# A hybrid decoder layer on one core: gate pieces moved between the recurrence levels, squares summed on TensorE, and a turned tile copied ahead of its unit

## The reference, cut to what matters

```python
x = x + 0.5 * swiglu(rms_norm(x, ffn1[0]), ...)        # d_ff = 2816
y = mixer_block(rms_norm(x, mix[0]), ...)
x = x + y
x = x + 0.5 * swiglu(rms_norm(x, ffn2[0]), ...)

# mixer_block
q, k, v, iq, ik, iw, hq, hf, hi, hg, ga, gb = split(h @ w_in)
attn = attend(q, k, v, iq, ik, iw)        # indexer picks 128 or 256 keys, softmax over these
o = hgrn2(silu(hq), sigmoid(-hf), log f, hi, s0)       # gated linear recurrence, 4 heads of 128 x 128
o = rms_norm(o) * silu(hg)
merged = sigmoid(ga) * (attn @ w_proj_attn) + sigmoid(gb) * (o @ w_proj_hgrn)
y = merged @ w_out
```

## Time and profile before

| | |
|---|---|
| three timed runs | 1734.11, 1739.26, 1740.22 us; median 1739.26 |
| the profiled execution, its own time | 1732.57 us |
| its span | 1730.5 us |
| mean granted clock of TensorE | 0.982 of full speed |
| busy: PE, PEld, DVE, ACT, POOL | 95%, 87%, 42%, 26%, 40% |
| chain that ended last | PE 89%, DVE 4%, ACT 2%, DMA 2% |
| HBM over the span | 116 GB/s |

### The profile page before, as it was taken

The page is one execution under the profiler, slowest core; times in us unless marked ns, Lnnn a source line. Parts: engine busy times, 40 slices in busy tenths (PEclk is TensorE's granted clock), DMA queues, the critical chain, the costliest instruction groups (busy, mean ns, idle before and its releaser), DMA issues.

```text
span 1730.5 us, 29178 instructions
## 1 busy us (share of the span) xinstructions
PE 1646.1 (95%) x12749; PEld 1512.9 (87%) x12753; DVE 732.0 (42%) x1190; ACT 445.7 (26%) x629; POOL 697.0 (40%) x584
## 2 busy tenths in 40 slices
PE   7999999999998899967999999998999999999998
PEld 6999999999957899956888765657999999999998
DVE  6323012334316589478574644435643222022311
ACT  4112111212452224300233333332233111111211
POOL 4333444446321245655144342341443434443432
PEclk9999999999999999988899999999999999999999
DMA  6222233423411223201522277998223222322222
GB/s 180 74 73 76 84 104 98 116 76 108 159 30 40 66 98 90 81 27 51 174 77 80 77 268 274 422 411 331 74 74 91 80 66 84 103 78 74 83 68 89
DMA packets 193502, 203.59 MB, mean 118 GB/s; under 512 B 6224, under 2 KB 179344, under 8 KB 184928
## 3 DMA queue, kind: packets, MB, share of 16 engines
q1 hardware_dynamic: 173040, 105.56, 21.3%
q0 software_dynamic: 12832, 80.29, 12.3%
q10 hardware_dynamic: 7504, 15.88, 2.4%
HBM read 187.21 MB, written 14.30 MB: 116 GB/s over the span
## 4 chain that ended last, share of the span: by engine, by line
PE 89%; DVE 4%; ACT 2%; DMA 2%; issue 1%; POOL 1%; ACTq 0%; SPq 0%; DVEq 0%; POOLq 0%
PE ps L1596 25%; PE ps L1597 24%; PE ps L1598 24%; PE ps L2048 3%; PE ps L2065 1%; PE ps L2123 1%; PE ps L1994 1%; DMA k_page<-in_cache_k,kv_row 1%; PE ps L2012 1%; PE ps L2003 1%; PE ps L1926 1%; DVE k_lev L1302 1%; DVE n_lo L1024 1%; PE ps L1609 1%; DVE att L1282 1%
## 5 line engine op out<-in xcount | busy, mean ns | idle before, releaser
L489 POOL TENSOR_TENSOR w_lo<-raw,w_hi 128x512 fp32r<-128x512 f32 (+1 forms) x398 | 525.9, 1351 | 784.1 <-ACT w_hi L642 784.1
L1596 PE MATMUL ps<-n_lo,w_hi 128*128 128x288 f32 x1824 | 544.0, 298 | 1.0 <-ACT qT L748 1.0
L1597 PE MATMUL ps<-n_hi,w_lo 128*128 128x288 f32 x1824 | 538.6, 295 | 0.0
L1598 PE MATMUL ps<-n_hi,w_hi 128*128 128x288 f32 x1824 | 536.8, 294 | 0.0
L1596 PEld LDWEIGHTS ps<-n_lo,w_hi 128*128 128x128 f32 x1824 | 342.4, 188 | 15.5 <-issue 14.4
L1598 PEld LDWEIGHTS ps<-n_hi,w_hi 128*128 128x128 f32 x1824 | 344.0, 189 | 0.0
L1597 PEld LDWEIGHTS ps<-n_hi,w_lo 128*128 128x128 f32 x1824 | 343.0, 188 | 0.1
L642 ACT ACTIVATE w_hi<-raw 128x2048 fp32r<-128x2048 f32 (+2 forms) x108 | 188.0, 1740 | 268.5 <-PE ps L1598 268.4
L1597 PE MATMUL ps<-hid_hi,w_lo 128*128 128x288 f32 x704 | 208.4, 296 | 0.0
L1596 PE MATMUL ps<-hid_lo,w_hi 128*128 128x288 f32 x704 | 208.4, 296 | 0.0
L1598 PE MATMUL ps<-hid_hi,w_hi 128*128 128x288 f32 x704 | 208.1, 296 | 0.0
(11 more groups left out here) (302 smaller groups left out, 2278.2 us busy)
## 6 DMA issues: line engine op xcount, KB each, us to landing
raw<-in_ffn_w_gate SPq DMA_DIRECT2D x44, 512.0 KB, 3.9
raw<-in_ffn_w_up SPq DMA_DIRECT2D x44, 512.0 KB, 5.2
raw<-in_ffn_w_down SPq DMA_DIRECT2D x32, 704.0 KB, 4.7
raw<-in_w_in SPq DMA_DIRECT2D x22, 1024.0 KB, 5.3
gates<-scratch_g ACTq DMA_DIRECT2D x4, 1152.0 KB, 9.8
raw<-in_w_out SPq DMA_DIRECT2D x4, 1024.0 KB, 5.1
scratch_g<-g_ring POOLq DMA_DIRECT2D x7, 576.0 KB, 3.1
scratch_x<-xT ACTq DMA_DIRECT2D x1, 2304.0 KB, 11.9
```

The source lines that it names most:

```text
L489: ins = pool.tensor_tensor(w_lo[:, u % NRAW, part], raw[:, u % NRAW, part], w_hi[:, u % NW, part].bitcast(F32), ALU.subtract)
L1596: pe.matmul(dst, hi, x_lo, start=first, stop=False)
L1597: pe.matmul(dst, lo, x_hi, start=False, stop=False)
L1598: return pe.matmul(dst, hi, x_hi, start=False, stop=last)
```

## The change

Five things are done, all in the order of instructions.

1. **Pieces between levels.** The 8 pieces of gate units 0 and 1 move from `prompt_attention` into the levels of `heads`: after each level of both heads PE makes half a piece (12 matmuls) in PSUM banks 0 to 3. ACT copies them out at the head of its `heads(g)`, SP stores them unscaled, and POOL scales that quarter (the last of the four, by `gate_quarter`) at the end, after it was loaded back. What stays in `prompt_attention` is two pieces ahead, a whole one in each of steps 0 to 13, and half a piece in each of steps 14 to 29.
2. **POOL's order.** `w_lo` of gate unit 1 is made after `decays(0)`, that of unit 2 after `decays(1)`, that of unit 3 after the last state store.
3. **The search.** Five of its rounds move from steps 11 to 15 to DVE's `heads(0)`, behind the first `level_in`.
4. **Squares.** PE adds up the squares of x itself: for every chunk two products with a matrix of ones, between the matmuls of `first_unit`. DVE's eight instructions on `sqsum` go, and PE's `norm(0)` too.
5. **Turned tile first.** In ACT's `token_major` the first turned tile of unit i-1 is copied before ACT waits for unit i, the second right after the stage copies and before `split`.

The diff, cut to its core:

```diff
+def gate_quarter(n):
+    return (n // 2 + 3) % 4
...
+        PRE, FULL = 2, 14
+        def piece_of_step(n):
+            return (2 * HB + PRE + n, (0, 1)) if n < FULL else (2 * HB + PRE + FULL + (n - FULL) // 2, ((n - FULL) % 2,))
         @block.sync
+            def store_piece(i):
+                sp.wait_ge(S("gate_out"), i + 1)
+                at = i % 4 * HT
+                sp.dma_start(g_home(i // 4)[:, at:at + HT], g_piece(i)).then_inc(S(f"head_stored{i % 3}"), 16)
             for u in range(NRAW, U):
+                n = u - NRAW - at_unit["gate", 0]
+                if n in (0, 1):
+                    for i in range(4 * n, 4 * n + 3):
+                        store_piece(i)
                 load_unit(u)
+                if n in (0, 1):
+                    store_piece(4 * n + 3)
         @block.gpsimd
-            lows(at_unit["feat", 5] + 2)
+            lows(at_unit["gate", 0])
...
             for g in range(2):
                 decays(g)
+                lows(at_unit["gate", g + 1])
                 state_store(2 * g)
                 state_store(2 * g + 1)
+            lows(at_unit["gate", 3])
             attention_pages()
...
+                pool.wait_ge(S("quarter_in3"), X_IN[3] + 16)
+                at = GATES_AT[3]
+                for n in range(2):
+                    for a in range(2):
+                        part = gates[:, at + n, a, :]
+                        ins = pool.tensor_tensor(part, part, rms[:, :], ALU.mult)
+                ins.then_inc(S("gate_scaled"), 1)
         @block.scalar
             def token_major():
                 for i in range(2, NTOK):
+                    if i > 2:
+                        turn_copies(TURNS_OF[i - 1][0:1])
                     act.wait_ge(S("unit_done"), u + 1)
...
                     ins.then_inc(S("stage_done"), 1)
+                    if i > 2:
+                        turn_copies(TURNS_OF[i - 1][1:])
                     split(u + 2)
                     if i == 2:
                         index()
-                    if i != 2:
-                        turn_out(i - 1)
+                    if i > 2:
+                        stored_out(i - 1)
             def heads(g):
+                for i in range(4 * g, 4 * g + 4):
+                    gate_out(i)
+            def stored_out(i):
+                act.wait_ge(S("tok_done"), i + 1)
+                for dst, src in stores(i):
+                    act.dma_start(dst, src).then_inc(S(f"stored{i % 2}"), 16)
             def gate_out(i):
...
+                if i % 4 == 3:
+                    split(at_unit["gate", n] + 2)
         @block.vector
-                for c in range(DC):
-                    sq_add(0, c)
...
+                        if h == 0 and L == 1:
+                            take(EARLY)
                         level_out(a, L - 1)
...
-                    if n < 16:
+                    if n < 16 - EARLY:
                         take(1)
         @block.tensor
             def first_unit(u):
+                def square(c):
+                    pe.wait_ge(S("sq_done"), c + 1)
+                    for h in range(2):
+                        ins = pe.matmul(ps[:, SS_BANK[0] + h, 0:HT], ones, sq[:, c % 2, h * HT:(h + 1) * HT],
+                                        start=c == 0, stop=c == DC - 1)
+                    ins.then_inc(S("sq_summed" if c < DC - 1 else "ss_done"), 1)
...
+                        if turn == 1 and k >= 2:
+                            square(k - 2)
+                        if turn == 2 and k < 2:
+                            square(DC - 2 + k)
             def second_unit(hi, lo):
-                norm(0)
-            def gate_half(i):
+            def gate_piece(i, part):
...
-                for k in range(DC):
+                for k in range(DC // 2 * part[0], DC // 2 * part[-1] + DC // 2):
             def heads(g):
                 for L in range(len(LEVELS)):
...
                         ins.then_inc(S(f"level_done{a}"), 1)
+                    gate_piece(4 * g + L // 2, (L % 2,))
             def prompt_attention():
-                    if n + 2 < 4 * HA:
-                        gate_half(n + 2)
+                    if piece_of_step(n)[0] < PIECES:
+                        gate_piece(*piece_of_step(n))
```

More of the change, by code:

```diff
@@ L82, in weight_units @@
         w_in("feat", 3 * g + 2, OHG + 256 * g, 256)
-    for g in range(DC // 2):
-        w_in("gate", 2 * g, OGA + 256 * g, 256)
-        w_in("gate", 2 * g + 1, OGB + 256 * g, 256)
+    for n in range(DC):
+        q = gate_quarter(n)
+        w_in("gate", n, (OGB if n % 2 else OGA) + 256 * q, 256)
     for g in range(DC // 2):
@@ L437, in build @@
         SMALL_IN = 16 * 8
+        X_IN = (32, 16, 16, 16)
         SCORE_AT = {2: 0, 3: 256, 4: 640}
@@ L525, in attention_pages @@
                 value_group(6)
-                for n in range(8):
+                for n in range(2, 8):
                     lows(min(at_unit["gate", n] + 2, at_unit["proj", 0]))
                     if n == 6:
-                        pool.wait_ge(S("gate_stored1"), 48)
+                        pool.wait_ge(S("gate_stored1"), 32)
                         value_group(5)
                     if n == 7:
-                        pool.wait_ge(S("gate_stored0"), 64)
+                        pool.wait_ge(S("gate_stored0"), 48)
                         value_group(4)
@@ L650, in squared @@
             def squared(k, c):
-                if DC * k + c >= 2:
-                    act.wait_ge(S("sq_added"), DC * k + c - 1)
+                n = DC * (k - 1) + c
+                if k == 0 and c >= 2:
+                    act.wait_ge(S("sq_summed"), c - 1)
+                if n >= 2:
+                    act.wait_ge(S("sq_added"), n - 1)
                 act.activation(sq[:, c % 2, :], xT[:, c, :], ACT.Square).then_inc(S("sq_done"), 1)
@@ L830, in gate_out @@
             def gate_out(i):
-                n, at = i // 4, i % 4 * HT
-                if i % 4 == 0:
-                    split(at_unit["gate", n] + 1)
+                n = i // 4
                 if i % 4 == 3:
@@ L885, in prompt_attention @@
                         turned(n - 1)
-                    if n + 1 < 4 * HA:
-                        gate_out(n + 1)
+                    if n == 0:
+                        gate_out(2 * HB + 1)
+                    elif piece_of_step(n - 1)[1][-1] == 1 and piece_of_step(n - 1)[0] < PIECES:
+                        gate_out(piece_of_step(n - 1)[0])
                     if n == 4 * HA - 1:
@@ L898, in prompt_attention @@
                 turned(4 * HA - 1)
-                split(at_unit["gate", 7] + 2)
             def sample_attention():
@@ L991, in _ @@
                     act.wait_ge(S("v_used"), 4 * (25 + g))
+                if g == 3:
+                    for m in range(3):
+                        act.wait_ge(S(f"head_stored{m}"), 16 * len(range(m, 2 * HB, 3)))
                 at = GATES_AT[g]
                 act.dma_start(gates[:, at:at + 2, :, :].rearrange("p n a t -> p n (a t)"),
-                              scratch_g[2 * g:2 * g + 2].rearrange("n p t -> p n t")).then_inc(S(f"gates_back{g}"), 16)
+                              scratch_g[2 * g:2 * g + 2].rearrange("n p t -> p n t")).then_inc(S(f"quarter_in{g}"), 16)
             act.dma_start(xT[:, :, :].rearrange("p c t -> p (c t)"), scratch_x).then_inc(S("x_back"), 16)
@@ L1181, in _ @@
             taken = [0]
+            EARLY = 5
             def take_half():
@@ L1573, in _ @@
             features(0)
-            while taken[0] < 2 * ROUNDS - 4 * HA:
+            while taken[0] < 2 * (ROUNDS - 16):
                 take_half()
@@ L1890, in features @@
                     ins.then_inc(S("unit_done"), 1)
-            def gate_half(i):
+            def gate_piece(i, part):
                 n, a, t = i // 4, i // 2 % 2, i % 2
                 hi, lo = unit(at_unit["gate", n])
-                if i >= 2:
-                    pe.wait_ge(S("gate_out"), i - 1)
-                for k in range(DC):
+                head = i < 2 * HB
+                if part[0] == 0 and i >= 4:
+                    pe.wait_ge(S("gate_out"), i - 3 if head else i - 1)
+                bank = i % 4 if head else 6 + t
+                for k in range(DC // 2 * part[0], DC // 2 * part[-1] + DC // 2):
                     at = k * 256 + a * P
-                    ins = product(ps[:, 6 + t, 0:HT], hi[:, at:at + P], lo[:, at:at + P],
+                    ins = product(ps[:, bank, 0:HT], hi[:, at:at + P], lo[:, at:at + P],
                                   n_hi[:, k, t * HT:(t + 1) * HT], n_lo[:, k, t * HT:(t + 1) * HT],
                                   k == 0, k == DC - 1)
-                ins.then_inc(S("unit_done" if i % 4 == 3 else "gate_half"), 1)
+                if part[-1] == 1:
+                    ins.then_inc(S("unit_done" if i % 4 == 3 else "gate_half"), 1)
             def heads(g):
```

61 lines of the change are left out of this document (37 added, 24 removed).

## The result

The changed kernel takes 1729.36 us in the median of four runs (1728.46 to 1729.93). The kernel before, timed beside it, takes 1739.74 (1734.11 to 1741.01). The ratio is 0.994, with a 95% interval of 0.9914 to 0.9967: 10.4 us faster, where 22.7 were forecast, and outside the forecast range of 1705 to 1728.

What follows compares the result with a forecast made beforehand. The prediction took TensorE (PE), 89% of the chain, as the bound. Terms 2.0 - 14.3 + 9.6 + 2.0 - 22.0 gave -22.7 us, taking the median 1739.26 to 1716.5 us, range 1705 to 1728.

Steps and rivals of the forecast that it cites:

- squares, up to the first token turn: First unit: PE's products with ones replace the 3.44 us wait but delay the second unit, +2.0 us (+1.0 to +4.1).
- turned tiles, units 3 to 5: Token units: three PE waits shrink from 3.72 to 0.95 us and lost clock returns, -14.3 us (-11 to -14.6).
- fourth turned tile: Before feature unit 0: ACT's later copies make PE wait 7.8 us, plus 1.8 of clock, +9.6 us (7.8 to 12).
- heads: Both heads stages: POOL's order, half pieces, clock and slowed DVE work together, +2.0 us.
- prompt_attention: Eight gate pieces of 3.32 us leave, less DVE's extra work then showing, -22.0 us (-26.5 to -17).
- steps don't shorten: Rival: in prompt_attention steps 14 to 29 the chain, not PE, sets the period; about 1730 us, chance 0.08.
- no room in the levels: Rival: every half piece in the heads levels pays in full, 26.4 us instead of 1.5; 1741.5 us, chance 0.05.
- They overrun by 2.1 us: Search in heads(0): five rounds, 13.0 us, against 10.9 us of DVE idle time left; hidden behind PE and POOL, 0 us.
- POOL's order -6.0, levels +1.5: Heads: decays lose the w_lo ahead of them, -6.0 us; half pieces exceed PE's idle time, +1.5 (0 to 4.6).
- The port, +5: Between levels and state blocks: DVE at half pace beside POOL's w_lo, 2.5 us late twice, +5 us (2 to 6).
- full lock: Rival: in heads DVE waits out whole w_lo instructions on the shared port, 10 us instead of 5; 1721.5 us, chance 0.10.
- Clock, +2 and -1: Heads: half pieces at low clock in heads(1), +2 us (0 to 4); busier PE loses less clock, -1 (0 to -6).

Runs made afterwards that it cites:

- e9: Kernel before the change with only the turned-tile edit, for the tiles behind token units 3, 4 and 5: 1721.74 us (0.9888).
- e2: Changed kernel, but ACT copies both turned tiles of token unit 6 behind token unit 7's stage copies and split: 1713.57 us (0.9844).
- e12: Changed kernel run again without any edit, for a second trace: 1724.25 us in a single run.
- e1: Changed kernel with the five search rounds back in steps 11 to 15 of prompt_attention: 1720.13 us (0.9898).
- e11: Changed kernel with the edits of e2 and e7, the five early search rounds kept in the levels: 1702.50 us (0.9768).
- e8: Changed kernel with three edits together, those of e1, e2 and e7: 1703.47 us (0.9802).
- e3: Changed kernel with the edits of e1 and e2 together: 1711.19 us (0.9844).
- e5: Kernel before the change run again without any edit, for a second trace: 1737.54 us.
- e7: Changed kernel with POOL's w_lo of gate units 1 and 2 held until DVE has made both v_own of the head pair: 1717.55 us (0.9881).
- e10: Changed kernel with ACT's old order of turned copies and without early search rounds, leaving gate pieces and squares: 1730.27 us (0.9900 to 0.9955).

## Why the prediction was wrong

Predicted terms against the means of the two traces of each kernel:

| step | predicted | measured |
|---|---|---|
| squares, up to the first token turn | +2.0 | +2.6 |
| turned tiles, units 3 to 5 (A) | -14.3 | -14.0 |
| fourth turned tile (B) | +9.6 | +9.2 |
| heads (E) | +2.0 | +12.9 |
| prompt_attention (F) | -22.0 | -21.6 |
| sample attention (G), rest | 0 | +2.7, +0.4 |
| sum | -22.7 | -7.8 |

The table accounts for the traces, whose spans lie 7.95 us apart on the mean; the medians of the timed runs lie 10.4 apart. The measured 1729.36 is just under 1730.6, the prediction's mark for a gain, so its class came true; its amount did not.

**Squares.** The second unit starts 1.1 us later in the first pair of traces (40.58 against 39.48) and 1.9 in the second (41.60 against 39.66), about as forecast. Counted from the start of the second turn of `first_unit` it is 16.27 and 16.28 us against 14.41 and 14.81, so 1.5 to 1.9 more; the rest is that start, which moves by some tenths from trace to trace. The rest of the 2.6 appears in the index stage: PEclk is at half for 7 us there where it was 3.4. The sum fits, the split was not foreseen.

**Turned tiles, fourth tile, prompt_attention.** Right in mechanism and size. e9 shows the first alone; in e2 B is 8.0 and 7.3 us shorter than in the two traces of the changed kernel without the fourth tile's order, as the 8.4 us wait said. In `prompt_attention` of e12 the steps with half a piece take 4.0 to 4.1 us for seven of them and 4.6 to 4.7 for the last, as forecast; the two steps with DVE's extra work, which have 3.4 us at half clock among them, take 6.3 and 6.2, 3.3 us more than the last ones, where the sum has 4.5. (Of the 1.9 in that sum, 7.2 less 4.6 less 0.9 is 1.7.) That the total agrees to 0.4 us is in part luck, since the clock in this stage differs between the two traces. The rivals *steps don't shorten* and *no fourth wait* are out by these rows, and *no room in the levels* by C of e1, which is 5.5 us shorter than before.

**heads is the step that failed**: +2.0 forecast, +12.9 measured. Of its four parts the first and the last below failed, the other two held.
- *"They overrun by 2.1 us, but the next level has to wait ... about as long. Nothing."* The lateness was mis-sized. I had DVE 3.7 us late; at the first `q_lev`, `k_lev` of the recurrence it was 10.4 late (722.62, where the kernel before was at 712.2). 4.5 came from the late start of the search, and 5.9 from bias and bound operations and one `q_lev` that the shift brought beside POOL's `w_lo`: 4.9 ahead of the second part of the search (rows under e2) and 1.0 behind it. The overrun was 7.9 us instead of 2.1. PE's half piece and POOL covered 1.9 of it, as forecast, and PE waited 5.97 for the rest. Together with the half clock behind that wait it cost 7 us of C (e1). The mechanism itself, rounds hidden behind PE, was right once DVE is in time (e11). The text named the case as one that would make it wrong, but gave it no chance of its own.
- *POOL's order -6.0, levels +1.5.* The sum is right: C without DVE's lateness (e1) is 32.8 instead of 38.3, -5.5. But the 10.2 us at half clock that C had before are gone too, so what the half pieces of `heads(0)` cost by themselves is not shown. In `heads(1)` the same stretch grew from 32.9 to 34.4 and 34.1 us, within the terms for the pieces and the low clock there.
- *The port, +5.* Right: D is 3.0 and 2.6 longer, 5.7 together. The rival of the full lock had 10. The Trainium skill (SBUF — State Buffer, "SBUF: two separate sides") says that VectorE in a two-port mode, or with two SBUF inputs beside a GpSimd operation that reads SBUF, and GpSimd lock each other out. The rows agree in kind: `k_lev` and `v_own`, each with two inputs, lost 1.07 and 1.54 us, POOL 2.56, and the PSUM readers nothing. My 5 us rested on half pace for POOL's whole time; it came out because `q_lev` (0.48 lost), `k_lev` and `v_own` are all that stood there.
- *Clock, +2 and -1.* Here the rest of the miss lies. Outside C and D, E grew by 8.0 in the first trace and 3.0 in the second: 3.4 and 3.6 in the state blocks of `heads(0)`, 1.5 and 1.2 in the levels of `heads(1)`, 3.1 and -1.8 behind them. I had let more work on PE mean less lost clock, and had no term for the state blocks of `heads(0)`, where the kernel before had 1 us at half clock and the changed one has 12 and 9. What brings it is not shown. The new waits (5.97, twice 2.8, 2.1) are the obvious candidate, and the wait at the first level fits: the half clock behind it is gone from C in e1. But in e8, where no wait around the turns of k is over 1.2 us, that part of `heads(0)` still has 10 us at half clock and is 3.7 us longer than before the change; and e2 and e3, with the same D, have 24 and 12. A test that holds the waits and changes the work between them was not made.

**The reference trace.** My sum started from an execution 7 us below the median, and I shifted it by that. The second trace places 4.8 of these us in the sample attention and behind, for which the sum has no term, so the shift was right. The 2.7 us of G in the table are mostly this one trace; about 1 remains (e5).

## What to carry to other kernels

Work put into an idle stretch of an engine must be paid from the idle time that is left after every earlier edit has moved that engine, and a late engine does not stay just as late: it slides beside another engine's work and can lose more there (5.9 of the 10.4 us here). So when one edit delays DVE (the fourth tile) and another spends its slack (the rounds), follow DVE's rows one by one from the first to the second, and price each at the duration that it has beside its new neighbour. Where a move puts POOL's SBUF work beside DVE's, try to hold POOL's with a wait until DVE's last SBUF-to-SBUF operation: here this was one line, took 6.2 us out of the two stretches D, and gave 11.8 us in e7 and 7.7 in e8 against e3.

## What the runs showed of the hardware

- Beside POOL's `w_lo`, DVE's `MAX8` and `MATCH_REPLACE8` over 1032 elements keep 1.24 and 1.22 us, and reads of PSUM their 0.72 and 0.35, while a `TENSOR_SCALAR` over 576 elements goes from 0.57 to 1.54 and a `TENSOR_TENSOR` over 576 from 0.75 to 1.82. So it depends on the operation whether DVE loses anything beside POOL.
- Two traces of one program can agree to 0.1 us in every stage up to the sample attention (before, e5), or have nearly the same waits and differ by 5 us in one stage, with 20 and 10 us at half clock (changed, e12). One trace doesn't tell which kind a kernel is.
- A pause of 2.8 us between the turns of k of the two heads of `heads(0)` stands in e2, e3 and e10 alike. In e2 and e10 one stretch of 21 us at half clock went with it; in e3 two of 3.4 us and then one of 10, with full clock between.
